# Two norms of a three-layer kernel: token sums as four columns, and the scale spread by diagonal products

## The reference, cut to what matters

```
# second layer: norm, modulation, mixer, gated residual
hx = modulate(rmsnorm(x, norm_g[1]), shift, scale)
x  = x + gate * odd_mixer(hx)
# end of the first block, start of the hybrid layer
x  = rmsnorm(x, final_g)
h  = rmsnorm_2(x, norm1_g)          # y = x * rsqrt(mean(x*x) + 1e-6) * g
u  = h @ w_in                       # q, k, v, conv, ssm, gates
...
x  = x + merged @ w_o
```

## Time and profile before

| | |
|---|---|
| median of 3 runs | 1797.67 us (1796.75 to 1798.75) |
| the profiled execution | 1793.85 us |
| its span (first to last instruction) | 1792.5 us |
| PE busy | 1715.0 us, 96% |
| PE weight loads busy | 1354.9 us, 76% |
| DVE busy | 959.5 us, 54% |
| ACT busy | 745.4 us, 42% |
| mean granted TensorE clock | 0.975 of full |

### The profile page before, as it was taken

How to read it: one execution, slowest core, us unless ns; L and a number is a source line. 1 busy time by engine, 2 the same in 40 slices (tenths; PEclk the granted TensorE clock), 3 DMA queues, 4 the chain that set the end, 5 groups by cost and what they waited for, 6 DMA issues and landing times.

```text
span 1792.5 us, 20062 instructions
## 1 busy us (share of the span) xinstructions
PE 1715.0 (96%) x8182; PEld 1354.9 (76%) x8182; DVE 959.5 (54%) x1300; ACT 745.4 (42%) x1012; POOL 18.9 (1%) x39
## 2 busy tenths in 40 slices
PE   6899999998999999999899989999999999999996
PEld 4788767675888888888587757776777788888885
DVE  4766566666657556644644453345555644444333
ACT  3587665656334333332333443433433423223221
POOL 0000000000000000000000000000000000000000
PEclk9899999999898999999899989999999999999998
DMA  7353545455232323222122211211222223222321
GB/s 318 120 173 133 163 144 175 141 178 176 83 104 72 106 95 106 94 94 95 58 96 69 79 40 59 82 64 54 71 83 95 94 94 101 99 94 95 106 94 47
DMA packets 54955, 190.13 MB, mean 106 GB/s; under 512 B 7312, under 2 KB 7312, under 8 KB 54608
## 3 DMA queue, kind: packets, MB, share of 16 engines
q1 hardware_dynamic: 47616, 159.52, 26.3%
q0 software_dynamic: 4848, 17.80, 3.0%
q10 hardware_dynamic: 2400, 11.53, 1.6%
HBM read 178.23 MB, written 2.10 MB: 101 GB/s over the span
## 4 chain that ended last, share of the span: by engine, by line
PE 83%; DVE 7%; ACT 6%; issue 2%; ACTq 1%; DMA 1%; DVEq 0%
PE banks L1436 24%; PE banks L1438 23%; PE banks L1437 23%; PE banks L1540 3%; PE banks L1468 2%; PE banks L1701 2%; ACT w_hi L409 2%; PE banks L1456 1%; PE banks L1723 1%; PE banks L1449 1%; DVE u L972 1%; PE banks L1745 1%; DVE w_lo L838 1%; PE banks L1791 1%; ACTq L435 1%
## 5 line engine op out<-in xcount | busy, mean ns | idle before, releaser
L1436 PE MATMUL banks<-h_hi,w_hi 128*128 128x512 f32 x1408 | 560.0, 398 | 9.2 <-DVE h_lo L847 5.0
L1438 PE MATMUL banks<-h_hi,w_lo 128*128 128x512 f32 x1408 | 552.0, 392 | 0.0
L1437 PE MATMUL banks<-h_lo,w_hi 128*128 128x512 f32 x1408 | 551.8, 392 | 0.0
L838 DVE TENSOR_TENSOR w_lo<-raw,w_hi 128x1024 fp32r<-128x1024 f32 x276 | 337.1, 1223 | 308.5 <-ACT w_hi L409 308.1
L409 ACT ACTIVATE w_hi<-raw 128x1024 fp32r<-128x1024 f32 x276 | 289.0, 1051 | 172.9 <-PE banks L1438 161.4
L1436 PEld LDWEIGHTS banks<-h_hi,w_hi 128*128 128x128 f32 x1408 | 266.3, 189 | 81.1 <-issue 19.1
L1438 PEld LDWEIGHTS banks<-h_hi,w_lo 128*128 128x128 f32 x1408 | 266.5, 189 | 57.0
L1437 PEld LDWEIGHTS banks<-h_lo,w_hi 128*128 128x128 f32 x1408 | 266.8, 189 | 53.7 <-issue 0.7
L1436 PE MATMUL banks<-y_hi,w_hi 128*128 128x512 f32 x192 | 76.9, 401 | 5.6 <-ACT gs L711 5.5
L1438 PE MATMUL banks<-y_hi,w_lo 128*128 128x512 f32 x192 | 75.7, 394 | 0.0
L1468 PEld LDWEIGHTS banks<-small,mraw 128*128 128x128 f32 x512 | 67.8, 209 | 10.4 <-DMA mraw<-modw 7.5
(11 more groups left out here) (342 smaller groups left out, 2151.3 us busy)
## 6 DMA issues: line engine op xcount, KB each, us to landing
raw<-weights SPq DMA_DIRECT2D x284, 512.0 KB, 3.2
mraw<-modw POOLq DMA_DIRECT2D x32, 512.0 KB, 4.7
mod<-modw ACTq DMA_DIRECT2D x4, 2048.0 KB, 23.1
rep<-U SPq DMA_DIRECT2D x96, 64.9 KB, 2.6
rep<-U SPq DMA_DIRECT2D x32, 64.8 KB, 2.4
X<-x_in ACTq DMA_DIRECT2D x1, 2048.0 KB, 13.6
out<-X SPq DMA_DIRECT2D x4, 512.0 KB, 2.7
ctx_x<-ctx_in ACTq DMA_DIRECT2D x1, 1024.0 KB, 19.9
```

What stands on the lines that cost most here:

```text
L838: tt(slot(w_lo, c), slot(raw, c), slot(w_hi, c).bitcast(F32), ALU.subtract).then_inc(S["lo"], 1)
L1436: mm(o, wh, r_hi, start=start, stop=False)
L1437: mm(o, wh, r_lo, start=False, stop=False)
L1438: return mm(o, wl, r_hi, start=False, stop=stop)
```

## The change

Three edits. **First**, the sum over features is turned round. `token_sum` takes the squares (128 tokens of them at a time) as the stationary operand and one column of ones as the moving one, so that a token's sum stands in a partition: 512 tokens are four columns. Root (ACT) and reciprocal (DVE) are taken on 128x4. To get the value back on all partitions, DVE multiplies the identity with each of the four columns (`token_scales`, four 128x128 tiles in `dg`, in the place of `rstd_b`), and PE multiplies a matrix of ones with each (`spread`), which leaves 128x512 in a PSUM bank; `norm_low` and the X pass read it from there. The last tile's squares are not added on DVE: PE sums `s1` (tiles 0 to 6) inside the last chunk, and `sqa` (tile 7) after it. For the pair of norms the moving operand has two columns (EPS and 1, or 1 and 0), so that s2 + EPS*s1 and s1 come out beside each other.

**Second**, PE takes the first two chunks after each of the two places together, tile by tile: six products for each `h_lo` tile, into two banks.

**Third**, order: the load of the root's table on ACT stands before the last square; PE's mod chunks are interleaved with the sums; the second spread of the pair of norms (`spread(2, 2)`), which the X pass needs, stands on PE after chunk ("qk", 0, 2), and DVE waits for it before the X pass. Some semaphores are renamed (`ores`, `wres`, `fres` into `res`, and so on), which changes no wait.

```diff
+        def token_scales(n, o):
+            e.wait_ge(S["f_sq"], n)
+            own.did(e.reciprocal(rc[:, o:o + NB], rc[:, o:o + NB]))
+            own.wait()
+            for j in range(NB):
+                ts(dg[:, j * P:(j + 1) * P], ident, rc[:, o + j:o + j + 1], None, ALU.mult).then_inc(S["dg"], 1)
...
# dve, before the hybrid layer
-        e.wait_ge(S["osum"], 2 * (NT - 1))
-        stt(s2[:, :], s1[:, :], EPS, s2[:, :], ALU.mult, ALU.add).then_inc(S["hsum"], 1)
-        inverse(5, r2)
-        norm_low(3, X, T, r2, lambda k: gn[:, k:k + 1], None, h_hi, h_lo, n_t2)
-        inverse(6, rstd2)
+        token_scales(5, 0)
+        e.wait_ge(S["rb"], 2)
+        norm_low(3, X, T, bank(3), lambda k: gn[:, k:k + 1], None, h_hi, h_lo, n_t2)
+        token_scales(6, NB)
+        e.wait_ge(S["rb"], 3)
         for k in range(NT):
-            own.did(stt(tile(X, k), tile(X, k), col("final_g", k), rstd2, ALU.mult, ALU.mult))
+            m = stt(tile(X, k), tile(X, k), col("final_g", k), bank(2), ALU.mult, ALU.mult)
...
# pe
+        def token_sum(b, total, w, start, stop):
+            n = w.shape[1]
+            for j in range(NB):
+                last = mm(bank(b, n, n * j), total[:, j * P:(j + 1) * P], w,
+                          start=start and j == 0, stop=stop and j == NB - 1)
+            return last
+
+        def spread(b, n):
+            for j in range(NB):
+                e.wait_ge(S["dg"], NB * n + j + 1)
+                last = mm(bank(b, P, j * P), ones, dg[:, j * P:(j + 1) * P], start=True, stop=True)
+            last.then_inc(S["rb"], 1)
...
-        for n in (28, 29):
-            mod_chunk(n, bank(BANK_OF[0], 2, 2 * n))
-        e.wait_ge(S["xsum"], NT - 1)
-        feature_sum(7, s1[:, :])
+        mod_chunk(28, bank(BANK_OF[0], 2, 56))
+        e.wait_ge(S["xsq"], NT)
+        token_sum(7, sqa[:, :], s_one, False, True).then_inc(S["fsum"], 1)
+        mod_chunk(29, bank(BANK_OF[0], 2, 58))
+        spread(6, 0)
         for n in (30, 31):
             mod_chunk(n, bank(BANK_OF[0], 2, 2 * n))
...
         def inputs_qkv(n):
             for t in range(4):
-                plain(("qk", n, t), sem=S["norm_lo"] if n == t == 0 else None, base=3 * NT)
-                yield
+                if n == 0 and t < 2:
+                    continue
+                plain(("qk", n, t))
+                yield
+                if n == 0 and t == 2:
+                    spread(2, 2)
...
+        c0, c1 = ready("qk", 0, 0), ready("qk", 0, 1)
+        b0, b1 = free("qk", 0, 0), free("qk", 0, 1)
+        for k in range(KC):
+            e.wait_ge(S["norm_lo"], 3 * NT + k + 1)
+            m0 = three(b0, c0, k, tile(h_hi, k), tile(h_lo, k), k == 0, k == KC - 1)
+            m1 = three(b1, c1, k, tile(h_hi, k), tile(h_lo, k), k == 0, k == KC - 1)
+        m0.then_inc(S["mm"], 1)
+        m1.then_inc(S["mm"], 1)
         run(inputs_qkv(0))
+        e.wait_ge(S["xfin"], 1)
```

More of the change, by code:

```diff
@@ L290, in program @@
     sg = [p(f"sg{k}", T) for k in range(4)]
-    rstd1, n_t1 = lev0[0][:, 0:T], [lev[:, T * k:T * (k + 1)] for k in range(3)]
+    n_t1 = [lev[:, T * k:T * (k + 1)] for k in range(3)]
     p = Plan(area2)
@@ L317, in program @@
     yt = [at(f"yt{k}", T, o_2 + 2 * K * k) for k in range(2)]
-    rstd2, r2, n_t2 = zs[:, 0:T], zs[:, T:2 * T], [bc[:, T * k:T * (k + 1)] for k in range(3)]
+    n_t2 = [bc[:, T * k:T * (k + 1)] for k in range(3)]
     tri_ones, after_m = cst2[:, 0:512], cst2[:, 512:640]
@@ L423, in root, with token_root @@
             fn(dst, bank(b, w), ACT.Sqrt, bias=eps, scale=1.0 / d).then_inc(S["f_sq"], 1)
+        def token_root(n, o, src, eps):
+            e.wait_ge(S["fsum"], n)
+            fn(rc[:, o:o + NB], src, ACT.Sqrt, bias=eps, scale=1.0 / D).then_inc(S["f_sq"], 1)
         def norm_high(q, w, hi_t, shift, tmps):
@@ L801, in act @@
             ahead("wo", f)
-            e.wait_ge(S["wres"], f + 1)
+            e.wait_ge(S["res"], 2 * NT + f + 1)
             if f > 1:
-                e.wait_ge(S["wsum"], f - 1)
-            fn(s1[:, :] if f == 0 else sqa[:, :], tile(X, f), ACT.Square).then_inc(S["wsq"], 1)
+                e.wait_ge(S["xsum"], NT - 2 + f - 1)
+            fn(s1[:, :] if f == 0 else sqa[:, :], tile(X, f), ACT.Square).then_inc(S["xsq"], 1)
             e.wait_ge(S["wg"], f + 1)
@@ L821, in act @@
                 ahead("fd", f, n)
-            e.wait_ge(S["fres"], f + 1)
+            e.wait_ge(S["res"], 3 * NT + f + 1)
             if f > 1:
-                e.wait_ge(S["fss"], f - 1)
-            fn(s1[:, :] if f == 0 else sqa[:, :], tile(X, f), ACT.Square).then_inc(S["fsq"], 1)
+                e.wait_ge(S["xsum"], 2 * NT - 3 + f - 1)
+            fn(s1[:, :] if f == 0 else sqa[:, :], tile(X, f), ACT.Square).then_inc(S["xsq"], 1)
         sqrt_table()
@@ L918, in dve @@
         own.did(e.memset(eps_ln, 4e-5))
+        own.did(e.memset(small[:, 388:389], EPS))
+        own.did(e.memset(small[:, 389:391], 1.0))
         e.memset(eps_sq, EPS * EPS).then_inc(S["eps"], 1)
@@ L1087, in dve @@
                 tt(s1[:, :], s1[:, :], sqa[:, :], ALU.add).then_inc(S["xsum"], 1)
-        inverse(4, rstd1)
-        norm_low(2, X, T, rstd1, lambda k: g1[:, k:k + 1], lambda k: modv1[:, k:k + 1], h_hi, h_lo, n_t1)
+        token_scales(4, 0)
+        e.wait_ge(S["rb"], 1)
+        norm_low(2, X, T, bank(6), lambda k: g1[:, k:k + 1], lambda k: modv1[:, k:k + 1], h_hi, h_lo, n_t1)
         e.wait_ge(S["mod_mm"], 32)
@@ L1153, in dve @@
             product("od", f, 1)
[L1154 to L1155 removed]
+            stt(tile(X, f), bank(f % 2), modv1[:, 16 + f:17 + f], tile(X, f), ALU.mult, ALU.add).then_inc(S["res"], 1)
+            if 0 < f < NT - 1:
                 e.wait_ge(S["osq"], 2 * f + 1)
@@ L1584, in pooled @@
                     e.wait_ge(S["lcp"], 4 * g + j - 1)
-                blocks(bank(j % 2), c, h_hi, h_lo, sem=S["norm_lo"] if g == j == 0 else None, base=2 * NT).then_inc(S["mm"], 1)
+                blocks(bank(j % 2), c, h_hi, h_lo).then_inc(S["mm"], 1)
             def gate(t):
@@ L1591, in gate @@
                 blocks(bank(2 + t % 2), c, h_hi, h_lo).then_inc(S["mm"], 1)
-            pooled(0)
-            pooled(1)
+            if g == 0:
+                c0, c1 = ready("u", 0, 0), ready("u", 0, 1)
+                for k in range(KC):
+                    e.wait_ge(S["norm_lo"], 2 * NT + k + 1)
+                    m0 = three(bank(0), c0, k, tile(h_hi, k), tile(h_lo, k), k == 0, k == KC - 1)
+                    m1 = three(bank(1), c1, k, tile(h_hi, k), tile(h_lo, k), k == 0, k == KC - 1)
+                m0.then_inc(S["mm"], 1)
+                m1.then_inc(S["mm"], 1)
+            else:
+                pooled(0)
+                pooled(1)
             gate(0)
```

78 lines of the change are left out of this document (49 added, 29 removed).

## The result

The changed kernel takes 1805.97 us (median of 6 runs, 1803.92 to 1807.70), the kernel before 1798.21 in its 6 runs (1796.23 to 1798.93). The ratio is 1.0046, 95% interval 1.0036 to 1.0056: slower by 8.3 us (6.5 to 10.1; the medians themselves differ by 7.8). Forecast were 1805.7, which is +8.05.

A forecast was written before the change was run, and what follows sets the result against it. PE, busy 96%, was taken to bound the kernel by its products, idle time and half clock. Terms +0.7 − 3.6 + 10.95 = +8.05 us on 1797.67 gave 1805.7 us; 8-in-10 range 1800.8 to 1809.5.

The forecast's parts named there:

- Behind B: After the norms before the hybrid layer: PE waits for a split queued behind the X pass, then half clock; +10.95 us.
- B in front: Norms before the hybrid layer, up to the first two qk chunks: earlier first tile, no waits between tiles; −3.6 us.
- The step that was off is the spread: Norms before the hybrid layer: only the last spread matmul charged, 0.2 to 0.4 us, behind diagonals of 0.90.
- PE's half clock after its first product: First products after the norms before the hybrid layer: 14 at half clock, 6.0 us, as in the trace before.
- A: Opening norm of the second layer: PE's last mod chunks end later, inside half clock; +0.7 us, bounds +0.4 and +1.3.
- the norm gains 1.7 us here: Opening norm of the second layer: first tile near 557.1, 1.7 us earlier, with no one waiting for it.
- mod chunk 29 and the spread: Opening norm of the second layer: chunk ends at 553.02 after two token sums, spread at 553.9 or 554.8 (half clock).
- The pair: First two qk chunks taken together: the 1.0 us PE spent waiting between tiles goes.
- The PSUM operand: X pass and norm_low reading their scale from PSUM: 0.06 us over eight instructions, taken as nothing.
- The clock did not stay up at A: Rival, opening norm of the second layer: clock stays at 1.00, mod chunks 30 and 31 take 3.5 us; 1798.8 us, 8%.
- DVE's first X product: Rival's sign, behind the pair: X pass starts before (qk,0,2) ends, so no stall; 1795.7 us, 3%.
- The third: Rival, whole kernel: late clock return, token sums at half clock, 6.8 us half clock after the stall; 1809.8 us, 12%.

The follow-up runs named there:

- e1: Changed kernel with DVE's splits of three chunks moved ahead of its wait for the second spread: 1795.87 us, 0.9988 of the kernel before.
- e10: Kernel before with only the second norms (before the hybrid layer) exactly as in the changed kernel, stall included: 1803.13 us, 1.0035.
- e5: Kernel before with the second norms as in the changed kernel, but DVE's three splits ahead of its wait: 1794.26 us, 0.9981.
- e3: Kernel before with one wait added: DVE starts the X pass only when PE has finished (qk,0,2): 1807.69 us, 1.0055.
- e2: Changed kernel with the second spread on PE ahead of chunk (qk,0,2) instead of behind it: 1799.75 us, 1.0005 of the kernel before.
- e8: e1 with mod chunks 30 and 31 both behind the first two u chunks: 1796.55 us, 0.9994 of the kernel before.
- e6: e1 with mod chunk 31 behind the first two u chunks: 1794.36 us, 0.9981 of the kernel before.
- e4: Kernel before with the change only at the opening norm of the second layer: 1797.60 us, 0.9998.
- e9: e5 with chunks (qk,0,0) and (qk,0,1) one after the other again: 1797.84 us, 1.0004 of the kernel before.
- e7: Kernel before with only chunks (qk,0,0) and (qk,0,1) taken together tile by tile: 1797.62 us, 1.0002.

## Why the prediction was right, step by step

**Behind B, the term that decides.** Forecast were 8.7 us from the end of ("qk", 0, 2) to PE's next product and 2.25 at half clock. Measured: 903.39 to 912.20, 8.8; and from there 7.47 to the copy at 919.67 where 5.44 is the price at full clock, 2.0. This is the mechanism as it was forecast, wait, releaser and size. Four comparisons of times give the stall without the spread's 0.9 us: 10.4 (e1), 9.7 (e10 to e5), 9.9 (e3), and with 5.4 us taken from the wait 7.4 of them are gone (e2). By traces it is 9.9, 10.0 and 9.7 (the same three pairs). The prediction has 10.1 for the same. The order of the two queues, read together, gave this; no row of before contains the stall.

**B in front, right in sum by luck: two errors cancel.** DVE's first product was forecast 2.6 us earlier against the end of the last od chunk as it was, bounds 1.5 and 2.6. It came 1.6 earlier: before it was 9.4 us behind that end (869.65 to 879.03), now it is 6.1 (876.93 to 883.00), of which 1.75 go back for the eight matmuls inside the chunk. The step that was off is the spread:

```profile
880.93 0.87 DVE L902 TENSOR_SCALAR rstd_b<-cst,small 128x128 f32<-128x128 f32 x4
```
```profile
881.28 1.70 PE banks L1488 x8
```

The prediction let three of its four matmuls run beside the diagonals and charged only the last. But PE starts with the first diagonal, 0.35 us after DVE does, and its four took 1.70 us, longer than DVE's 0.87; the clock fell at 881.73, among them. On the other side, PE's half clock after its first product lasted from 885.28 to 888.56, 3.3 us and not the 6.0 of the earlier trace rows. The low stretch itself was as long as before, 6.8 us (881.73 to 888.56, and before 880.48 to 887.3). But before PE came to its first product 0.8 us after the clock fell, and now 3.55 us after it, so that less of the stretch fell on products. The 48 products took 12.7 us, against 14.7 before and 13.7 in the forecast.

```profile
881.73:888.56 6.83, 4.51 (x15) 3.57 (x14) 5.60 (x10) 2.74 (x5) 0.00 (x0) 0.50 0.04 17
```

Where the fall lies differs between traces. With columns and the pair, the front takes 99.7 (after, e2), 99.8 (e10), 100.8 (e5), 100.9 (e8), 101.0 (e6) and 102.5 us (e1). Without them it takes 102.8 (e3), 103.2 (before) and 103.3 (e4). The means differ by 2.5 us. The -3.5 of this pair of traces is the upper end, and -2.5 is the forecast's own weak bound.

**A, direction right, size too small.** Forecast +0.7 within 0.4 and 1.3; in this pair of traces +2.5, over ten traces +1.2. That PE's mod chunks come last is as named: the norm's first `h_lo` is ready at 562.42, 4.2 us before PE starts its u chunks at 566.58. But the step "the norm gains 1.7 us here" did not hold in this trace. Counted from the first result, `h_lo` comes 49.5 us after it, and 48.9 before: what the reciprocal saved, DVE spent waiting for a spread that stood on PE behind mod chunk 29. In e1, where 29 ran at full clock, it comes after 46.9, 2.0 earlier, and no one waits for it either. The price is that the clock fell at 554.05 here, before mod chunk 29; PE starts its u chunks 3.2 us later than before, and not 1.3:

```profile
554.63 3.55 PE L1508 MATMUL banks<-small,mraw 128*128 128x2 f32 x16
...
558.04 2.06 PE L1488 MATMUL banks<-rstd_b,cst 128*128 128x128 f32 x8
...
566.58 0.77 PE L1461 MATMUL banks<-h_hi,w_hi 128*128 128x512 f32 x1
```
```profile
560.14 1.40 DVE L922 SCALAR_TENSOR_TENSOR lev<-X,small,banks 128x512 f32<-128x512 f32 x2 [3.95 <-PE banks L1488]
561.67 0.75 DVE L929 SCALAR_TENSOR_TENSOR h_lo<-lev,small,h_hi 128x512 fp32r<-128x512 f32 x1
```

Sixteen records in 3.4 us is a mod chunk at half clock; the forecast had 29 at full clock, because it was in the trace of before. I had taken from one trace where the clock falls in relation to the work. The traces since show that it moves: against the first L1082 the fall comes 42.9 us later before, 41.2 after, 44.0 in e1 and 41.1 in e2. The clock's fall should have had a bound of its own, of one mod chunk in either direction. The term mis-sized is therefore the one for mod chunk 29 and the spread, priced at or near full clock: 29 took 3.4 us for the 1.7 of the sum.

**The pair.** The 1.0 us of waits between tiles was there: e5 has none but the first, and e9, without the pair, waits for tiles 0.8 us more. That more than this needs the splits out of the way (e7) was not in the prediction.

**The total.** That 8.05 meets 8.3 so closely is in part luck. In the ledger the terms of the sum add up to +9.8 (2.5 - 3.5 + 10.8) where 8.05 were forecast, A being 1.8 too small, and the rest, which had no term, gives 1.3 back. The term that carries the result, 10.8 of it, was right by itself.

**The PSUM operand.** Forecast: nothing. The X pass of the changed kernel has 742 ns an instruction, with the scale in PSUM:

```profile
L1191 DVE SCALAR_TENSOR_TENSOR X<-X,vec,banks x8: 742/742/748, 904.3 to 908.9; 128x512 f32<-128x512 f32 x8
```

Before, the same eight took 5.39 us, now 5.36. The 65 ns more (an estimate from its table) that the Trainium skill's page "VectorE: DVE Perf Modes" (section on the TRN2 errata) would put on it are not there. Nor are the 25 ns, an estimate from the same table, for a matmul of one column: four token-sum matmuls took 0.81 us in the last chunk of the first layer (548.78 to 549.59), and eight of two columns 1.70 in the last od chunk (869.48 to 871.18), 0.20 and 0.21 each, as the mod chunks'.

**The rivals.** The clock did not stay up at A (0.50 from 554.05 to 571.12). DVE's first X product did not start before ("qk", 0, 2) ended. The third, all clock terms at their bad ends, came true for A only. A fourth, tested in e1, would have put the loss on the added matmuls; without the stall they cost less than the columns and the pair gain.

## What to carry to other kernels

Before moving the point at which an engine waits, list what is queued behind the waiting instruction, down to the next thing that the other engine needs: here a pass of DVE over `X`, which nobody reads again before 1385 us, was made to wait for PE, and a weight split that PE needed at once stood behind it, 10 us for three instructions in the wrong order. Where an edit makes the busiest engine arrive earlier at a later point, the small cover that its helpers had there shrinks by as much (about 1 us of cover before, none and a wait of 0.91 in e7). Shorten a chain only where the timeline shows that the busiest engine waits for it: of two identical edits one met a PE that was waiting (B) and gained, the other one that was busy with something else (A) and cost about 1. Before reading an effect of 1 to 3 us from times, look whether the clock behind the edit is the same in both traces.

## What the runs showed of the hardware

Fp32 matmuls with a fresh 128x128 stationary operand cost 0.20 to 0.22 us at full clock whether one or two columns move, 0.43 at half with two (a mod chunk of eight in 3.41 us, 554.63 to 558.04), and with 128 columns 0.23 at full clock (the two qk chunks behind the pair take 11.8 us in e1 with four such matmuls between them, and 10.9 before without); each shows as two records; so here turning a sum round into columns makes the vector engines' part small (a reciprocal of 128x4 takes 0.18 us against 3.35 for 128x512) and PE's part not smaller: eight such matmuls take longer than the 1.10 us of the 512-column sum they replace.

Half-clock stretches depend on more than the local code. PE fully busy with mod chunks ran at 0.50 for 6.7 us (559.9 to 566.6 in the changed kernel, and 6.84 in the earlier trace rows), so that such matmuls did not bring the clock back here. Kernels that differ by a microsecond in one place had or had not such a stretch some 15 us later (e9 against e5, e7 against before). For effects of 1 to 3 us in this kernel, a stretch between two events of the trace, over several traces, told more than the times did.
